# Hybrid decoder layer on one core: the order of small TensorE products between the wide weight products, and two moved steps around them

## The chip, the core and the metric

The kernel runs on one NeuronCore of a Trainium2 chip, in one launch. The metric is the device time of that core in microseconds (us), as the median of several runs.

## What is computed

One layer (DEPTH = 1) of a decoder, for 256 prompt tokens and 8 sample sequences of 4 tokens (32 sample tokens, so 288 token columns in all), with width 2048. Cut to what matters here:

```
proj = a @ w_in                                  # HGRN2 q,f,i,g | delta net q,k,v,z | gates
# HGRN2, 16 heads, chunks of 32 tokens, per chunk:
o = A @ i + (q*exp(G)) @ S ;  S = exp(G_last)*S + (k*exp(G_last-G))^T @ i
# gated delta net, 32 heads in 16 pairs, chunks of 64 tokens, per chunk:
X = solve(A + I, rhs)                            # triangular, unit diagonal
v_new = u - w @ S ;  o = (q*exp(gam)) @ S + attn @ v_new ;  S = exp(g_last)*S + k^T @ v_new
# then output projections, residuals, and a feed-forward part with w_up and w_down
```

The sample sequences start from given states (`state_hgrn`, `state_gdn`), so each head also has 8 products of one sample state with 4 tokens.

## The kernel before

All weights stream from HBM once. A weight piece of 128 x 512 is split by ScalarE into a rounded high part (`whi`, line 1036) and by VectorE into the rest (`wlo`, line 1530), and TensorE makes three products for each 128 x 128 tile of it: `whi` with the high part of the activations, `whi` with their low part, and `wlo` with the high part (lines 609, 610, 611), each 288 columns wide. These are called wide weight products here. SyncE issues the weight loads. A slab is 16 tiles of one block of 128 output rows, that is 48 wide weight products.

The small products of the two recurrences are put between them. `products` calls `between(s)` before every second tile, so a step s is followed by six wide weight products. One head of HGRN2 lasts four slabs (steps 0 to 31), one pair of delta-net heads six slabs (steps 0 to 47). While the projection of head i+1 is made, the steps of head i run (`hgrn_steps`, `delta_second`), together with those that prepare head i+1 (`delta_first`). ScalarE and VectorE have lists of steps by the same numbers (`delta_prev` and `delta_own` on each), with a split of a weight piece at every even step, in the order of the program. GpSimd (POOL) has its own order. So what an engine does is fixed by hand; semaphores say when.

All the small products have ordinary fp32 operands. Each shows in the trace as two MATMUL records and two LDWEIGHTS records; the two are called halves here. A transpose through TensorE shows one of each.

In the delta net the triangular inverse is built in levels. For level l = 1 to 5, TensorE makes PU (steps 4, 8, 11, 14, 17; line 799: the level's matrix with `g_Ui`), ScalarE copies it (line 1276), TensorE makes UT (steps 6, 10, 13, 16, 19; line 812: `g_PU` with `g_T`), VectorE subtracts it from `g_Ui` (line 1890) and transposes that to `g_T` (line 1893). PU of level l+1 waits for the subtraction of level l (`g_unew`). GpSimd makes the matrix of the level (`g_lev`, line 2338). At level 1 the samples have two 32 x 32 products more in PU (line 802) and in UT (line 815), subtracted in line 1889. Step 8 has four sample products of 32 columns (lines 823, 825), and steps 9 to 12 the sixteen of 8 columns with the sample states (line 833). When these are done (`g_sw`), GpSimd scales the states (line 2355, twice), after its level 5, which waits for PU of level 3. Step 16 starts with the sum of squares of the next head's keys or queries (line 742), which waits for ScalarE's square (line 1227) of what lines 1794 and 1795 on VectorE wrote; before these VectorE has line 1881, level 3 and the split of step 12.

In VectorE's step 5, `silu_z` (line 1872) multiplies two 128 x 288 arrays in SBUF for the output gate; in its own step 5 line 1774 copies the halo of the convolution (lines 1784 and 1787, step 10).

In HGRN2, step 0 transposes six blocks and makes the in-chunk products (lines 667, 668), step 10 the value products (683, 685), steps 11 to 14 the sixteen halves of 4 columns with the sample states (689), and steps 15 and 16 the chunk products (695).

## Time and profile before

| | |
|---|---|
| median of 3 runs | 3562.6 us (3562.56 to 3563.32) |
| the profiled execution's own time | 3563.5 us |
| its span from first to last instruction | 3562.0 us |
| mean granted TensorE clock | 0.994 |
| TensorE matmuls busy | 3481.4 us, 98% |
| TensorE weight loads busy | 3176.9 us, 89% |
| VectorE, ScalarE, GpSimd busy | 63%, 50%, 24% |
| HBM | 545.83 MB read, 40.99 MB written, 165 GB/s |

The profiled execution took 1.5 us more than its span, and stands 0.9 us above the median. The busy time of matmuls is modelled and overlaps from one to the next, so it doesn't say how much of it could go. The start times of the weight loads (engine PEld) do: in a stream of products there is one load for each product. HGRN2's heads run from about 187 to 745 us, the delta net's from about 998 to 1546 and from 1754 to 2350.

### The profile page before, as it was taken

Reading aid. Unit: us, or ns where it says so; the run is one execution under the profiler, and the core shown is the slowest. Engines: PE = TensorE matmul, PEld = TensorE weight load, DVE = VectorE, ACT = ScalarE, POOL = GpSimd, SP = SyncE. Lnnn points to the kernel's source line nnn. Section 1 sums busy time; section 2 is a strip of 40 time slices with the busy share of each in tenths; the row PEclk is TensorE's granted clock in tenths of the full one; section 3 lists DMA queues with packets and bytes.
Section 4 is the critical chain, followed back from the end, with each engine's and each line's share of the span. In section 5 each row is a group of like instructions: output and inputs, shape, how many; then the busy total and the mean of one; then the engine's idle time right before and its main releaser. Section 6 shows DMA issues by size and latency. Waiting matters only on the chain.

```text
span 3562.0 us, 76760 instructions
## 1 busy us (share of the span) xinstructions
PE 3481.4 (98%) x24605; PEld 3176.9 (89%) x24605; DVE 2252.7 (63%) x4307; ACT 1796.9 (50%) x3735; POOL 845.4 (24%) x995
## 2 busy tenths in 40 slices
PE   8999999999999999999999999999998999999998
PEld 2599999998889999998899999899878989999998
DVE  2476666746677777776677777646666665555555
ACT  1245454555545545556555555454665555444444
POOL 2122222201144554441244455412000000000000
PEclk9999999999999999999999999999999999999999
DMA  8655555568843433448744343468764785555554
GB/s 276 215 150 157 147 160 145 156 180 258 251 114 111 116 109 109 123 119 240 211 116 128 109 115 110 112 184 247 232 199 130 216 238 163 168 159 169 161 165 138
DMA packets 884546, 588.09 MB, mean 165 GB/s; under 512 B 23426, under 2 KB 816036, under 8 KB 884164
## 3 DMA queue, kind: packets, MB, share of 16 engines
q1 hardware_dynamic: 857828, 510.50, 50.0%
q0 software_dynamic: 26624, 76.41, 7.5%
q8 instruction: 50, 0.82, 0.1%
q14 instruction: 44, 0.36, 0.0%
HBM read 545.83 MB, written 40.99 MB: 165 GB/s over the span
## 4 chain that ended last, share of the span: by engine, by line
PE 93%; DVE 3%; issue 2%; DMA 1%; ACT 1%; DVEq 0%; POOL 0%; ACTq 0%; SPq 0%; POOLq 0%
PE acc L609 23%; PE acc L611 22%; PE acc L610 22%; PE acc L581 3%; PE bank L799 2%; PE bank L812 2%; PE bank L849 2%; PE bank L833 1%; PE bank L621 1%; PE bank L622 1%; DMA raw<-in_w_ada 1%; PE bank L870 1%; PE bank L674 1%; PE bank L676 1%; DVE wlo L1530 1%
## 5 line engine op out<-in xcount | busy, mean ns | idle before, releaser
L1530 DVE TENSOR_TENSOR wlo<-raw,whi 128x512 fp32r<-128x512 f32 x1799 | 1302.8, 742 | 828.9 <-ACT whi L1036 815.3
L1036 ACT ACTIVATE whi<-raw 128x512 fp32r<-128x512 f32 x1799 | 1094.8, 627 | 840.7 <-PE acc L611 799.5
L609 PE MATMUL acc<-ahi,whi 128*128 128x288 f32 x4112 | 1288.8, 313 | 14.5 <-DVE alo L2041 9.1
L610 PE MATMUL acc<-alo,whi 128*128 128x288 f32 x4112 | 1215.3, 296 | 0.0
L611 PE MATMUL acc<-ahi,wlo 128*128 128x288 f32 x4112 | 1211.4, 295 | 0.0
L609 PEld LDWEIGHTS acc<-ahi,whi 128*128 128x128 f32 x4112 | 775.5, 189 | 37.1 <-issue 26.2
L610 PEld LDWEIGHTS acc<-alo,whi 128*128 128x128 f32 x4112 | 776.6, 189 | 13.3 <-issue 11.5
L611 PEld LDWEIGHTS acc<-ahi,wlo 128*128 128x128 f32 x4112 | 775.9, 189 | 0.0
L609 PE MATMUL acc<-ohi,whi 128*128 128x288 f32 x1792 | 533.2, 298 | 3.9 <-ACT g_C L1045 3.3
L610 PE MATMUL acc<-olo,whi 128*128 128x288 f32 x1792 | 529.4, 295 | 0.0
L611 PE MATMUL acc<-ohi,wlo 128*128 128x288 f32 x1792 | 527.9, 295 | 0.0
L609 PEld LDWEIGHTS acc<-ohi,whi 128*128 128x128 f32 x1792 | 336.7, 188 | 22.6 <-DVE wlo L1530 10.0
L610 PEld LDWEIGHTS acc<-olo,whi 128*128 128x128 f32 x1792 | 337.0, 188 | 2.8
L611 PEld LDWEIGHTS acc<-ohi,wlo 128*128 128x128 f32 x1792 | 337.9, 189 | 0.0
L2338 POOL TENSOR_TENSOR g_lev<-g_A,levm 128x512 f32<-128x512 f32 x80 | 114.1, 1426 | 282.6 <-DVE g_C L1795 219.3
L1276 ACT ACTIVATE g_PU<-bank 128x512 f32<-128x512 f32 x80 | 47.8, 598 | 175.1 <-PE bank L799 164.4
L1787 DVE SCALAR_TENSOR_TENSOR g_ca<-g_U,g_cw,g_ca 128x312 f32<-128x312 f32 x192 | 131.8, 687 | 6.8
L581 PE MATMUL acc<-raw,cst 128*9 128x512 f32 x256 | 115.9, 608 | 7.0 <-DMA raw<-in_w_ada 4.4
L1890 DVE TENSOR_TENSOR g_Ui<-g_Ui,bank 128x512 f32<-128x512 f32 x80 | 54.7, 683 | 80.4 <-PE bank L812 80.4
L621 PE MATMUL bank<-whi,cs 128*18 128x512 f32 x256 | 101.3, 396 | 3.4 <-DVE wlo L1530 2.5
L799 PE MATMUL bank<-g_Ui,g_lev 128*128 128x128 f32 x640 | 87.9, 280 | 16.6 <-DVE g_Ui L1890 13.6
L581 PEld LDWEIGHTS acc<-raw,cst 128*9 128x9 f32 x256 | 22.4, 92 | 90.5 <-issue 70.7
(431 smaller groups left out, 4412.2 us busy)
## 6 DMA issues: line engine op xcount, KB each, us to landing
raw<-in_w_in SPq DMA_DIRECT2D x386, 512.0 KB, 4.1
raw<-in_w_ada SPq DMA_DIRECT2D x192, 512.0 KB, 4.6
raw<-in_w_up SPq DMA_DIRECT2D x128, 512.0 KB, 4.2
raw<-in_w_down SPq DMA_DIRECT2D x128, 512.0 KB, 4.0
raw<-in_w_out_gdn SPq DMA_DIRECT2D x64, 512.0 KB, 5.0
raw<-in_w_o SPq DMA_DIRECT2D x34, 512.0 KB, 4.7
raw<-in_w_out_hg SPq DMA_DIRECT2D x32, 512.0 KB, 5.5
g_S<-in_state_gdn POOLq DMA_DIRECT2D x32, 512.0 KB, 6.6
```

What stands on the lines that cost most here:

```text
L581: last = mm(acc[c % 2][0:NC, :], cst[:, 2 * l + a, :], raw[:, 2 * (l % 4) + a].rearrange("p k c -> p (k c)"), start=(l + a == 0), stop=(l ...
L609: mm(bank[:, 0:T], whi[:, s, r, :], hi[:, kt, :], start=(kt == 0), stop=False, skip_group_check=True)
L610: mm(bank[:, 0:T], whi[:, s, r, :], lo[:, kt, :], start=False, stop=False, skip_group_check=True)
L611: last = mm(bank[:, 0:T], wlo[:, s, r, :], hi[:, kt, :], start=False, stop=(kt == KT - 1), skip_group_check=True)
L621: mm(R[4][0:2 * NC, :], cs2[:, kt, :], whi[:, s].rearrange("p k c -> p (k c)"), start=(kt == 0), stop=False)
L799: last = mm(R[3][:, p * P:(p + 1) * P], glev[:, l % 2, p, :], gUi[:, p, :], start=True, stop=True)
L812: last = mm(R[2][:, p * P:(p + 1) * P], gT[:, p, :], gPU[:, p, :], start=True, stop=True)
L849: last = mm(R[4 + a][:, :], gkls[:, e, :], gvX[:, 4 * a:4 * a + 4, :].rearrange("p b v -> p (b v)"), start=True, stop=True)
L1036: f(whi[:, s], raw[:, r], ACT.Copy).then_inc(sg["hi_made"], 1)
L1530: tt_(wlo[:, s], raw[:, r], whi[:, s].bitcast(F32), SUB).then_inc(sg["lo_made"], 1)
L1787: stt(gca[:, 0:CW], gU[:, k, a:a + CW], gcw[:, k, a:a + 1], gca[:, 0:CW], MUL, ADD).then_inc(sg["g_part" if a < 3 else "g_tap"], 1)
L2338: last = pt(glev[:, l % 2], gA[:, :, :], levm[:, l, :].unsqueeze(1).to_broadcast([P, 4, P]), MUL)
```

## The change

It moves instructions; it adds and removes none but waits and signals. On TensorE:

- Level 1 of PU and of UT: the two 32 x 32 products, which were last, now stand after the first and after the second of the four large ones.
- The products of the decay matrices (step 31 of `delta_first`): the two products of 32 rows, which were last, now stand second.
- Step 0 of HGRN2: the 32 x 32 output block (line 668) and the two sample transposes now stand after the first transpose; the in-chunk products of the prompt end the step.
- The x transposes of the output stage: the one of 32 rows stands second of three.
- Step 8 of the delta net stands in front of PU of level 2 (it stood behind it).
- The sixteen products with sample states: ten halves at step 10 in front of UT of level 2, twenty-two at step 11 in front of PU of level 3 (before: 10, 6, 6, 10 halves at steps 9, 10, 11, 12, those of 10 and 11 behind the level product).
- HGRN2: all of step 10 to 14 in step 10, with a product of 128 columns last; steps 15 and 16 both in step 16.
- Step 37 of the delta net (output): one of the prompt's value products stands last, for each of the two heads.

On VectorE `silu_z` moves from step 5 to step 7. On GpSimd the first load of the sample states of the delta net (`load_delta(0)`) is issued after the last merged rows are stored, where it was before that loop.

```diff
 hgrn_steps, s == 0
                     for a in range(2):
                         turn(R[2][:, a * P:(a + 1) * P], hX[:, 3, a * P:(a + 1) * P], ident[:, :])
+                        if a == 0:
+                            mm(R[4][0:NS, TP:T], hX[:, 1, TP:T], hX[:, 0, TP:T], start=True, stop=True)
+                            turn(R[3][0:NS, 0:P], hX[:, 3, TP:T], ident[:, :])
+                            turn(R[3][0:NS, P:2 * P], hi_[:, TP:T], ident[:, :])
                         turn(R[2][:, (2 + a) * P:(3 + a) * P], hi_[:, a * P:(a + 1) * P], ident[:, :])
-                    turn(R[3][0:NS, 0:P], hX[:, 3, TP:T], ident[:, :])
-                    turn(R[3][0:NS, P:2 * P], hi_[:, TP:T], ident[:, :])
...
 hgrn_steps, s == 10
+                    pe.wait_ge(sg["h_s0"], 16 * (n + 1))
+                    mm(R[7][:, 0:P], htok[:, 2, :], hAT[:, 0:P], start=True, stop=False, skip_group_check=True)
                     mm(R[7][:, TP:T], htoks[:, 1, :], hAT[:, TP:T], start=False, stop=False, skip_group_check=True)
-                if s in (11, 12, 13, 14):
-                    pe.wait_ge(sg["h_s0"], 16 * (n + 1))
-                    for b in range(2 * s - 22, 2 * s - 20):
+                    for b in range(NB):
...
+                    mm(R[7][:, P:2 * P], htok[:, 3, :], hAT[:, P:2 * P], start=False, stop=False, skip_group_check=True)
-                if s in (15, 16):
-                    first, end = ((1, 5), (5, NHC))[s - 15]
-                    pe.wait_ge(sg["h_step"], 8 * n + end - 1)
+                if s == 16:
+                    pe.wait_ge(sg["h_step"], 8 * n + NHC - 1)
...
 delta_second: the step 8 block and the state products, now in front of PU and UT
+                if s in (10, 11):
+                    if s == 10:
+                        pe.wait_ge(sg["g_qw"], n + 1)
+                        pe.wait_ge(sg["g_s0"], 32 * (n + 1))
+                    for i in range(*((0, 5), (5, 2 * NB))[s - 10]):
...
                     for p in range(4):
                         last = mm(R[3][:, p * P:(p + 1) * P], glev[:, l % 2, p, :], gUi[:, p, :], start=True, stop=True)
-                    if l == 1:
-                        for e in range(2):
-                            last = mm(R[5][0:NS, e * NS:(e + 1) * NS], glevs[:, e, :], gUs[0:NS, e, :], start=True, stop=True)
+                        if l == 1 and p < 2:
+                            mm(R[5][0:NS, p * NS:(p + 1) * NS], glevs[:, p, :], gUs[0:NS, p, :], start=True, stop=True)
...
                     for p in range(4):
                         last = mm(R[2][:, p * P:(p + 1) * P], gT[:, p, :], gPU[:, p, :], start=True, stop=True)
-                    if l == 1:
-                        for e in range(2):
-                            last = mm(R[4][0:NS, e * NS:(e + 1) * NS], gTs[:, e, :], gPUs[:, e, :], start=True, stop=True)
+                        if l == 1 and p < 2:
+                            mm(R[4][0:NS, p * NS:(p + 1) * NS], gTs[:, p, :], gPUs[:, p, :], start=True, stop=True)
...
-                if s in (9, 10, 11, 12):
-                    if s == 9:
...
-                    for i in range(*((0, 5), (5, 8), (8, 11), (11, 2 * NB))[s - 9]):
...
 VectorE, delta_prev
-                if s == 5:
+                if s == 7:
                     silu_z(2 * n + 2, 1)
...
 GpSimd
-            load_delta(0)
             with pool.Fori(KT // 2 - 2, KT // 2) as n:
                 merged_out(n)
...
+            load_delta(0)
             pool.wait_ge(sg["g_halo_turned"], 1)
```

## Rows read from the trace of the kernel before

**Rows 1.** The page: busy us (share of the span) x instructions of TensorE.

```profile
PE 3481.4 (98%) x24605; PEld 3176.9 (89%) x24605; DVE 2252.7 (63%) x4307; ACT 1796.9 (50%) x3735; POOL 845.4 (24%) x995
```

**Rows 2.** Waits of TensorE: us in total, times, longest.

```profile
PE bank L799 <- DVE g_Ui L1890: 13.6, 15, 1.5
```

**Rows 3.** Timeline of the weight loads, step 12: start, us, instruction.

```profile
1331.68 1.21 PEld L833 LDWEIGHTS bank<-g_QW,g_S 128*128 128x128 f32 x10
1332.81 0.19 PEld L609 LDWEIGHTS acc<-ahi,whi 128*128 128x128 f32 x1
```

**Rows 4.** Timeline of the weight loads, step 6 (UT of level 1).

```profile
1318.39 0.99 PEld L812 LDWEIGHTS bank<-g_PU,g_T 128*128 128x128 f32 x8
1319.50 0.20 PEld L815 LDWEIGHTS bank<-g_PUs,g_Ts 32*32 32x32 f32 x4
1319.74 0.19 PEld L609 LDWEIGHTS acc<-ahi,whi 128*128 128x128 f32 x1
1319.84 0.19 PEld L610 LDWEIGHTS acc<-alo,whi 128*128 128x128 f32 x1
```

**Rows 5.** Timeline of the weight loads, HGRN2 step 0.

```profile
319.00 0.14 PEld L663 LDWEIGHTS bank<-ident,h_i 128*128 128x128 f32 x1
319.11 0.10 PEld L664 LDWEIGHTS bank<-ident,h_X 128*32 128x32 f32 x1
...
319.33 0.53 PEld L667 LDWEIGHTS bank<-h_X 128*128 128x128 f32 x4
319.98 0.14 PEld L668 LDWEIGHTS bank<-h_X 128*32 128x32 f32 x2
320.15 0.19 PEld L609 LDWEIGHTS acc<-ahi,whi 128*128 128x128 f32 x1
```

**Rows 6.** Timeline of VectorE, steps 4 to 6 of the same head as rows 4.

```profile
1318.26 1.78 DVE L1530 TENSOR_TENSOR wlo<-raw,whi 128x512 fp32r<-128x512 f32 x1 [2.06 <-ACT whi L1036]
1319.96 1.54 DVE L1872 TENSOR_TENSOR g_z<-g_ca,g_ce 128x288 f32<-128x288 f32 x1
...
1321.72 0.67 DVE L1890 TENSOR_TENSOR g_Ui<-g_Ui,bank 128x512 f32<-128x512 f32 x1
```

**Rows 7.** Timeline of the weight loads in front of step 8: same head, last head.

```profile
1321.18 0.19 PEld L611 LDWEIGHTS acc<-ahi,wlo 128*128 128x128 f32 x1
1322.50 0.30 PEld L799 LDWEIGHTS bank<-g_Ui,g_lev 128*128 128x128 f32 x2 [1.14 <-issue]
...
2280.02 0.19 PEld L611 LDWEIGHTS acc<-ahi,wlo 128*128 128x128 f32 x1
2281.90 0.30 PEld L799 LDWEIGHTS bank<-g_Ui,g_lev 128*128 128x128 f32 x2 [1.69 <-issue]
```

**Rows 8.** Timeline of GpSimd, levels 3, 4 and 5, then the state scaling.

```profile
1319.46 1.72 POOL L2338 TENSOR_TENSOR g_lev<-g_A,levm 128x512 f32<-128x512 f32 x1
...
1323.75 1.28 POOL L2338 TENSOR_TENSOR g_lev<-g_A,levm 128x512 f32<-128x512 f32 x1 [1.04 <-PE bank L799]
...
1330.60 1.58 POOL L2338 TENSOR_TENSOR g_lev<-g_A,levm 128x512 f32<-128x512 f32 x1 [1.80 <-PE bank L799]
1333.06 3.76 POOL L2355 TENSOR_TENSOR g_S<-g_S,g_sc 128x1024 f32<-128x1024 f32 x2 [0.88 <-PE bank L833]
```

**Rows 9.** Timeline of VectorE, steps 10 to 13.

```profile
1329.92 2.60 DVE L1787 SCALAR_TENSOR_TENSOR g_ca<-g_U,g_cw,g_ca 128x312 f32<-128x312 f32 x3
...
1334.80 0.69 DVE L1890 TENSOR_TENSOR g_Ui<-g_Ui,bank 128x512 f32<-128x512 f32 x1 [1.17 <-PE bank L812]
...
1336.16 1.21 DVE L1530 TENSOR_TENSOR wlo<-raw,whi 128x512 fp32r<-128x512 f32 x1
```

**Rows 10.** Timeline of the weight loads around step 16.

```profile
1338.15 0.19 PEld L611 LDWEIGHTS acc<-ahi,wlo 128*128 128x128 f32 x1
1338.57 0.30 PEld L742 LDWEIGHTS bank<-g_ns,ones 128*128 128x128 f32 x2 [0.23 <-issue]
```

**Rows 11.** VectorE in the last head's step 5, with no next head behind it.

```profile
2276.28 3.09 DVE L1872 TENSOR_TENSOR g_z<-g_ca,g_ce 128x288 f32<-128x288 f32 x1
```

More of the change, by code:

```diff
@@ L681, in hgrn_steps @@
                     pe.wait_ge(sg["h_t1"], n)
-                    for a in range(2):
-                        mm(R[7][:, a * P:(a + 1) * P], htok[:, 2 + a, :], hAT[:, a * P:(a + 1) * P], start=(a == 0), stop=False,
-                           skip_group_check=True)
+                    pe.wait_ge(sg["h_s0"], 16 * (n + 1))
+                    mm(R[7][:, 0:P], htok[:, 2, :], hAT[:, 0:P], start=True, stop=False, skip_group_check=True)
                     mm(R[7][:, TP:T], htoks[:, 1, :], hAT[:, TP:T], start=False, stop=False, skip_group_check=True)
-                if s in (11, 12, 13, 14):
-                    pe.wait_ge(sg["h_s0"], 16 * (n + 1))
-                    for b in range(2 * s - 22, 2 * s - 20):
+                    for b in range(NB):
                         mm(R[7][:, TP + b * TS:TP + (b + 1) * TS], hS0[:, b, :], hX[:, 2, TP + b * TS:TP + (b + 1) * TS],
                            start=False, stop=False, skip_group_check=True)
-                if s in (15, 16):
-                    first, end = ((1, 5), (5, NHC))[s - 15]
-                    pe.wait_ge(sg["h_step"], 8 * n + end - 1)
-                    for c in range(first, end):
+                    mm(R[7][:, P:2 * P], htok[:, 3, :], hAT[:, P:2 * P], start=False, stop=False, skip_group_check=True)
+                if s == 16:
+                    pe.wait_ge(sg["h_step"], 8 * n + NHC - 1)
+                    for c in range(1, NHC):
                         last = mm(R[7][:, c * HC:(c + 1) * HC], hS[:, c - 1, :], hX[:, 2, c * HC:(c + 1) * HC], start=False,
                                   stop=(c == NHC - 1), skip_group_check=True)
-                    if s == 16:
-                        last.then_inc(sg["h_o"], 1)
+                    last.then_inc(sg["h_o"], 1)
                 if s == 19:
@@ L788, in delta_second @@
                     last.then_inc(sg["g_qk_turned"], 1)
+                if s == 8:
+                    pe.wait_ge(sg["g_unew"], 5 * n + 1)
+                    pe.wait_ge(sg["g_tokd"], EARLIER + n + 1)
+                    pe.wait_ge(sg["g_halo"], halos)
+                    for e in range(2):
+                        mm(R[7][:, e * NS:(e + 1) * NS], gbek[:, 2, e, :], gUs[:, e, :], start=True, stop=True)
+                    for e in range(2):
+                        last = mm(R[7][:, 64 + e * NS:64 + (e + 1) * NS], gbv[:, 2, e, :], gUs[:, e, :], start=True, stop=True)
+                    last.then_inc(sg["g_uts"], 1)
+                if s in (10, 11):
[3 more added lines that the diff above has]
+                    for i in range(*((0, 5), (5, 2 * NB))[s - 10]):
+                        e, b = i // NB, i % NB
+                        last = mm(R[4][:, 64 * e + 8 * b:64 * e + 8 * b + 8], gS0[:, e, b, :],
+                                  gQW[:, e, b].rearrange("p k t -> p (k t)"), start=True, stop=True)
+                    if s == 11:
+                        last.then_inc(sg["g_sw"], 1)
                 if s in PU:
@@ L890, in delta_second @@
                         bank = (R[7], R[4])[e]
-                        for a in range(2):
-                            mm(bank[:, a * P:(a + 1) * P], gvn[:, a, e, :], gat[:, a, e, :], start=(a == 0), stop=False, skip_group_check=True)
+                        mm(bank[:, 0:P], gvn[:, 0, e, :], gat[:, 0, e, :], start=True, stop=False, skip_group_check=True)
                         mm(bank[:, TP:T], gvns[:, e, :], gats[:, e, :], start=False, stop=False, skip_group_check=True)
                         for c in range(1, NGC):
-                            last = mm(bank[:, c * GC:(c + 1) * GC], gS[:, c - 1, e, :], gqpT[:, e, c * GC:(c + 1) * GC],
-                                      start=False, stop=(c == NGC - 1), skip_group_check=True)
+                            mm(bank[:, c * GC:(c + 1) * GC], gS[:, c - 1, e, :], gqpT[:, e, c * GC:(c + 1) * GC],
+                               start=False, stop=False, skip_group_check=True)
+                        last = mm(bank[:, P:2 * P], gvn[:, 1, e, :], gat[:, 1, e, :], start=False, stop=True, skip_group_check=True)
                     last.then_inc(sg["g_o"], 1)
@@ L938, in x_turn @@
                         for a in range(2):
-                            turn(R[5 + k % 2][:, a * P:(a + 1) * P], xin[:, a, c], ident[:, :])
-                        turn(R[5 + k % 2][:, TP:T], xin[0:NS, 2, c], ident[0:NS, 0:NS]).then_inc(sg["w_xturned"], 1)
+                            last = turn(R[5 + k % 2][:, a * P:(a + 1) * P], xin[:, a, c], ident[:, :])
+                            if a == 0:
+                                turn(R[5 + k % 2][:, TP:T], xin[0:NS, 2, c], ident[0:NS, 0:NS])
+                        last.then_inc(sg["w_xturned"], 1)
                 for k in range(MIXED_SLABS):
```

29 lines of the change are left out of this document (7 added, 22 removed).

## The prediction

> **What bounds the kernel now.** I read the page first, then TensorE's waits, then, where the change is, the timelines of the weight loads, VectorE and GpSimd. On the page TensorE's matmuls are busy 98% of the span and VectorE 63% [rows 1]. So each slot on TensorE counts, and work elsewhere counts only where TensorE waits for it. The list of waits has one line that bears on the change: 13.6 us in 15 waits of L799 for L1890 [rows 2]. Busy time can't tell what an order of products costs, since matmul records overlap; the starts of the weight loads can, as each product has one. I take them as the clock of TensorE.
>
> **Narrow products, and bursts of them.** Ten loads of L833, each for a product of only 8 columns, take 1.13 us up to the next load [rows 3]: 0.113 us each. The eight of L812, 128 columns wide, go at the same pace: the eighth starts some 0.78 us after the first [rows 4]. So a narrow product costs one load, 0.11 us, whatever is in front of or behind it. A burst that ends with 8 columns leaves the next wide weight product's load visible; one that ends with 128 columns has the load under the product, but takes 0.11 us for it as well. In rows 3 the wide product's load follows the last narrow one like any other. I cost at nothing: HGRN2's steps 10 to 16, the sixteen state products put in two bursts, the wide product last in step 37, and the order in step 31 and of the x transposes, which have one change of shape before and one after. If a boundary of a burst has a cost that I miss, say 0.01 us, it is 16 x 7 boundaries, 1 us, of either sign. The wide product that now signals step 37's end is 64 columns longer than L895's, half of a 0.11 us slot, 0.05 us; step 40 waits for what follows from it, so 16 x 0.05 = +0.8 us.
>
> **The 32-row products.** In UT of level 1 the eighth L812 load would start at 1318.39 + 0.13 + 6 x 0.112 = 1319.19 and the next at 1319.30, but L815's starts at 1319.50: 0.20 us late. Its four halves follow each other 0.03 us apart, and L609's load comes 0.24 us after the first. L610's follows 0.10 us later, a load that nothing covers [rows 4]. Without L815, L609 would start at 1319.30 and not at 1319.74: the four halves cost 0.43 to 0.44 us. The same shape of cost stands in HGRN2, for two halves: the last of four L667 loads starts at about 319.66, L668's should follow at 319.77, and L609's comes at 320.15 [rows 5], so 0.38 us for two. So most of the cost is the change of shape, once in and once out, and not the product: two halves more add 0.06 us. The change puts the pair of the first head behind the first large product and that of the second behind the second, with a large one between: two changes in and two out. Two pairs apart cost 2 x (0.435 - 0.06) = 0.75 us, against 0.435: +0.315 us. With PU and UT of level 1 in 16 head pairs, 32 x 0.315 = **+10.1 us**. Bounds: nothing, if the change of shape is free inside a burst; 2 x 0.38 - 0.435 = 0.33 us by HGRN2's row, +10.6 us. I take the first, as it has the same shape. Nothing hides it: UT's end sets level 1's subtraction, and TensorE has work up to it.
>
> The Trainium skill (TensorE: Matmul & The Clock Gate, Step-by-step: what each phase is for) says that a weight load is pulled ahead of matmuls in flight if the row groups don't conflict or the load goes to the background buffer. By that the 32-row load would go under the large product, and this term would be 0. The late L815 load [rows 4] speaks against it here.
>
> In HGRN2's step 0 the number of changes stays one, but behind L668 comes L664, with 32 columns to load in place of 128. L664 follows L663 with no gap, 0.11 us [rows 5]. The exposed load behind L668 should shrink from 0.10 to about 0.03 us, the pace of the 32-column loads of L815: 15 x -0.07 = -1.1 us, between that and 0.
>
> **Step 8 and silu_z.** In front of step 8's L799, the last wide load is at 1321.18; L799's is due at 1321.31 and comes at 1322.50: a gap of 1.19 us [rows 7]. It waits for L1890, 1321.72 to 1322.39, which stood behind L1872, in VectorE's queue: 1319.96 to 1321.50 [rows 6]. L1872 reads two arrays in SBUF and took 1.54 us, as POOL's L2338 ran to 1321.18 [rows 8]. With L1872 in step 7, VectorE has only the halo copy between the split that ends at 1320.04 and UT's end. UT ends about 0.63 us later by the term above (0.315 twice), at about 1320.4. From L1872's end to L1890's, halo copy included, are 0.89 us (1321.50 to 1322.39), so L1890 ends by 1321.3, and L799 is due at 1321.31 + 0.63 = 1321.94. The gap goes, with 0.6 us to spare. The load starts show such a gap in 13 heads, 0.87 to 1.22 us, 14.8 us in all, and in two heads none; the list's 13.6 us [rows 2] counts idle time from modelled ends, some 0.25 us short for each. In the last head the gap is 1.75 us [rows 7]: there L1872 took 3.09 us [rows 11] and the split of step 6 stands behind it; some 1.5 of it should go. Sum **-16.3 us**. Bounds: 0 if L1890 is held by something else, -17.5 by the list with 0.26 added to each wait. The step 8 products now stand in front of L799 and wait for the same signal, so this order alone would gain nothing. L1872 is next used at step 42; in its new place it is behind the split of step 6, and the pieces are three ahead.
>
> **Level 3 and step 16.** What is late next is GpSimd. Now L2338 of level 5 starts at 1330.60 when PU of level 3 is done, and the scaling L2355 waits for the last state product, 1333.06 to 1336.82 [rows 8]. VectorE's split of step 12 reads two SBUF arrays; it starts at 1336.16 and ends at 1337.37, 0.55 us after L2355 ends, and took 1.21 in place of 0.69 [rows 9]. L1794, L1795 and L1227 follow, and L742 of step 16, due at 1338.28, comes at 1338.57 [rows 10]. So TensorE already waits 0.29 us there, and a later end of L2355 is paid in full. After the change PU of level 3 stands behind 22 halves and not 6: relative to UT of level 2, 16 x 0.112 = 1.79 us later. L2338 starts at 1332.39. VectorE's three L1787 (2.60 us, the last held by L2338 [rows 9]) are then done, so it takes 1.28 us as in level 4 [rows 8], to 1333.67. The signal for L2355 is there already; two of 1.90 us (3.76 overlapped) end at 1337.43: 0.6 us later than 1336.82, while UT of level 3, which VectorE's split follows, stays where it is. L742 has a next head in 15 heads: 15 x 0.58 = **+8.7 us**. Bounds: 0 if the split gets in between the two L2355, and 15 x 1.0 if L2338 takes 1.72. I take the middle, since the split is asked for in the middle of the second L2355, before as after.
>
> The Trainium skill (SBUF — State Buffer, Who interferes with whom) says that a VectorE instruction with two SBUF inputs and a GpSimd one that reads SBUF hold each other off for a whole instruction. With that rule the wait lasts to the end of the second L2355, as in my sum; if they only shared bandwidth, the term would be nearer to 2 us.
>
> The other levels keep their waits: between UT and the next PU of levels 3 and 4 there is one step before as after. UT of level 3 now has only 12 wide products between it and PU, for ScalarE's copy, as UT of level 1 has before too, and that one comes without a gap [rows 2, 4]. HGRN2's step 16 waits for VectorE's last state step, which the list of waits doesn't show now, and it is put no earlier. load_delta(0) is issued later, but its states are first used in step 10 of the second stretch of six slabs, 6 x 48 x 0.13 = 37 us after the first: 0.
>
> **Sum.** +0.8 + 10.1 - 1.1 - 16.3 + 8.7 = +2.2 us, with some 0.5 for boundaries +2.7. Against the profiled execution's 3563.5 us (span 3562.0 and 1.5 around it) that is 3566.2; the median before is 0.9 lower, so **3565.3 us**.
>
> **Rivals.** (a) The second change of shape is free: without the 10.1, 3555.2. For it: no row shows a 32-row product in front of a large fp32 one. Against: L609's load behind L815 waits for the same thing. (b) No later L742: without the 8.7, 3556.6. For it: it rests on when two queues meet. (a) and (b) together: 3546.5. (c) Slower: L2338 of level 5 starts at 1332.39, and VectorE's split of step 10 at about 1331.7 (0.9 earlier than L1787's end now, without the hold), done at 1332.4. If it starts later than L2338, they meet, L2338 takes 1.58 to 1.72 us as in rows 8, and L742 comes 0.3 to 0.44 us later still: +4.5 to +6.6 us, 3569.8 to 3571.9. It decides from 0.3 us on. (d) The gap at step 8 stays because L1890 is held by L2338 itself and not through L1872: 3565.3 + 16.3 = 3581.6. Against: L1890 took 0.69 us at 1334.80 while L2355 ran [rows 8, 9]. (e) The change does nothing that can be seen since its parts cancel: that is nearly my forecast.
>
> **Chances.** 0.2% is 7.1 us, about what a measurement of this kernel can tell from no change. My forecast 0.42, (a) 0.14, (b) 0.15, (a) with (b) 0.06, (c) 0.16, (d) 0.03, others 0.04. Faster by over 0.2% (below 3555.5): (a), both, some of the forecast's and (b)'s lower side, 0.27. Slower (above 3569.7): (c), (d) and a part of the forecast's upper side, 0.22. The same: 0.51. The range leaves out (a) with (b), and (d): 3551 to 3573; my forecast's own is 3560 to 3570.
>
> **What the profile after would show.** L799's wait for L1890 near nothing, and L1872 at 0.45 us. L802 and L815 in groups of two, each behind a gap of 0.2 us, and 0.37 us for each. L2355 ending 0.6 us later against UT of level 3, and L742's gap at 0.87 us in place of 0.29. If L742 comes no later or a group of two costs under 0.1 us, I am too high; if L799 still waits at step 8, too low.

## The result, and the profile after

The changed kernel takes 3574.5 us (median of 7 runs, 3570.9 to 3576.1) where the kernel before takes 3562.6 (7 runs, 3558.7 to 3566.6). The ratio is 1.0032, with an interval of 1.0020 to 1.0043: 11 to 12 us slower, where I had forecast 3565.3, no measurable change, and a range of 3551 to 3573. The profiled execution took 3570.9 us with a span of 3569.4, so it is the fastest of the seven, 7.4 us above the one before. Of the executions of all the kernels below, one stood apart (h0_back, 3641.8 us at a mean granted clock of 0.916), and its ratio leaves it out.

The page's busy row, to set beside [rows 1]:

```profile
PE 3491.1 (98%) x24605; PEld 3181.5 (89%) x24605; DVE 2213.3 (62%) x4307; ACT 1793.7 (50%) x3735; POOL 848.2 (24%) x995
```

Instruction counts are the same; VectorE is busy 40 us less: 17 of it are L1872, which no longer meets L2338, 15 the convolution (L1787) and 12 the splits, which meet GpSimd less often too, and other lines have a little more. TensorE's waits, as in [rows 2] (line numbers are those of the changed kernel: L818 is PU, old L799; L740 is old L742; L676 is old L674; L899 is old L901):

```profile
PE bank L740 <- ACT g_ns L1227: 6.4, 11, 0.6
...
PE bank L676 <- POOL h_iXs L2201: 3.8, 13, 0.3
PE bank L899 <- DVE wlo L1530: 3.5, 14, 0.3
...
PE bank L818 <- DVE g_Ui L1890: 2.0, 2, 1.4
```

Of the 15 waits of [rows 2] those at step 8 are gone. Of the two left for L1890, both in the last head, one of 0.7 us was there before, and one of 1.4 us is new (see below). L740's wait is the one I had forecast. The waits of L676 and L899 I had not.

**Level 1.** The weight loads of step 6, the same head as [rows 4]:

```profile
1324.46 0.32 PEld L830 LDWEIGHTS bank<-g_PU,g_T 128*128 128x128 f32 x2
1324.90 0.13 PEld L832 LDWEIGHTS bank<-g_PUs,g_Ts 32*32 32x32 f32 x2
1325.08 0.30 PEld L830 LDWEIGHTS bank<-g_PU,g_T 128*128 128x128 f32 x2
1325.49 0.13 PEld L832 LDWEIGHTS bank<-g_PUs,g_Ts 32*32 32x32 f32 x2
1325.67 0.52 PEld L830 LDWEIGHTS bank<-g_PU,g_T 128*128 128x128 f32 x4
1326.11 0.19 PEld L609 LDWEIGHTS acc<-ahi,whi 128*128 128x128 f32 x1
```

From the first load to the last group of four are 1.21 us, of which the four large loads in between are 0.45: 0.76 for two pairs apart, where four halves together cost 0.435 [rows 4]. L832 comes some 0.2 us late both times, behind large products of its own burst.

**Step 8.** VectorE has only the split and the halo copy in front of UT's end; its timeline:

```profile
1326.71 0.67 DVE L1890 TENSOR_TENSOR g_Ui<-g_Ui,bank 128x512 f32<-128x512 f32 x1
1327.41 0.71 DVE L1893 STREAM_TRANSPOSE g_T<-g_Ui 128x512 f32<-128x512 f32 x1
1328.05 0.65 DVE L1530 TENSOR_TENSOR wlo<-raw,whi 128x512 fp32r<-128x512 f32 x1
1328.62 0.45 DVE L1872 TENSOR_TENSOR g_z<-g_ca,g_ce 128x288 f32<-128x288 f32 x1
```

L1890 is done at 1327.38, before the first product of step 8 is due at 1327.67, and that comes on time. L1872 takes 0.45 us and not 1.54 [rows 6].

**Step 16.** GpSimd's levels 4 and 5 and its scaling, as in [rows 8]:

```profile
1329.83 1.29 POOL L2338 TENSOR_TENSOR g_lev<-g_A,levm 128x512 f32<-128x512 f32 x1 [1.33 <-PE bank L818]
...
1337.58 1.28 POOL L2338 TENSOR_TENSOR g_lev<-g_A,levm 128x512 f32<-128x512 f32 x1 [2.69 <-PE bank L818]
1338.83 3.74 POOL L2355 TENSOR_TENSOR g_S<-g_S,g_sc 128x1024 f32<-128x1024 f32 x2
```

and the loads around L740, as in [rows 10]:

```profile
1343.36 0.19 PEld L611 LDWEIGHTS acc<-ahi,wlo 128*128 128x128 f32 x1
1344.33 0.30 PEld L740 LDWEIGHTS bank<-g_ns,ones 128*128 128x128 f32 x2 [0.78 <-issue]
```

L740 is due at 1343.49 and comes at 1344.33: a gap of 0.84 us, 0.29 before. Level 5's L2338 takes 1.27 to 1.29 us in all 16 heads, where it took 1.58 to 1.61 in 15 of them before: the meeting of rival (c) doesn't come.

**Step 14 of the last head** takes 1.3 us longer (3.52 and not 2.22), which I had not forecast. Behind the moved state products GpSimd's scaling now starts 0.22 us ahead of VectorE's split of step 12, where before it started 0.34 us behind it:

```profile
2301.82 4.20 POOL L2355 TENSOR_TENSOR g_S<-g_S,g_sc 128x1024 f32<-128x1024 f32 x2
```

```profile
2302.04 2.22 DVE L1530 TENSOR_TENSOR wlo<-raw,whi 128x512 fp32r<-128x512 f32 x1 [4.23 <-ACT whi L1036]
```

```profile
2305.11 0.97 PEld L818 LDWEIGHTS bank<-g_Ui,g_lev 128*128 128x128 f32 x8 [1.59 <-DVE wlo L1530]
```

The split takes 2.22 us and not 0.69, the subtraction of level 3 (L1890) stands behind it, and PU of level 4 (L818) waits for that. states_only below has the same 1.3 us.

**HGRN2, the first surprise.** Per head, step 8 of HGRN2 takes 4.36 us in 13 of 16 heads, the third to the fifteenth (from the first product of one step's weight stream to that of the next), and 3.83 in all but the first before. Here are GpSimd and then VectorE in such a head (the fifth) of the kernel before:

```profile
321.92 2.49 POOL L2199 TENSOR_TENSOR h_iX<-h_tok,cm 128x512 f32<-128x512 f32 x2 [5.73 <-ACT h_toks L1135]
324.37 1.89 POOL L2201 TENSOR_TENSOR h_iXs<-h_toks,cm 32x1024 f32<-32x1024 f32 x1
```

```profile
322.81 0.70 DVE L1530 TENSOR_TENSOR wlo<-raw,whi 128x512 fp32r<-128x512 f32 x1 [0.47 <-ACT whi L1036]
324.42 3.80 DVE L1530 TENSOR_TENSOR wlo<-raw,whi 128x512 fp32r<-128x512 f32 x3 [0.90 <-ACT whi L1036]
```

and in the changed kernel:

```profile
322.20 2.49 POOL L2199 TENSOR_TENSOR h_iX<-h_tok,cm 128x512 f32<-128x512 f32 x2 [5.74 <-ACT h_toks L1135]
324.65 2.39 POOL L2201 TENSOR_TENSOR h_iXs<-h_toks,cm 32x1024 f32<-32x1024 f32 x1
```

```profile
322.99 0.79 DVE L1530 TENSOR_TENSOR wlo<-raw,whi 128x512 fp32r<-128x512 f32 x1 [0.38 <-ACT whi L1036]
324.59 0.69 DVE L1530 TENSOR_TENSOR wlo<-raw,whi 128x512 fp32r<-128x512 f32 x1 [0.80 <-ACT whi L1036]
```

Before, L2201 starts 0.05 us ahead of the split of step 4 and the split is held. After, the split starts 0.06 us ahead of L2201, and L2201 is the one that is held: 2.39 us and not 1.89. The product of step 8 (L676), which waits for it, is 0.5 us late. Step 0 became 0.09 us shorter, as forecast (-0.07); the split follows the products of the first slab and so comes that much earlier, while L2201 hangs on ScalarE's copies and doesn't. Counted from the last wide load ahead of step 0, the split starts after 5.80 us and not 5.89, and L2201 after 5.85 us in both kernels. In the second head of the same execution the order is still the old one (L2201 starts 0.04 us ahead, takes 1.89), and its step 8 takes 3.83.

**The clock, the second surprise.** Windows of the changed kernel: stretch, us, busy time of TensorE, weight loads, VectorE, ScalarE, GpSimd (instructions), granted clock, DMA share, GB/s. The first two are of the third delta net head, the other two of the fifth:

```profile
1182.40:1185.90 3.50, 3.50 (x33) 3.50 (x33) 3.36 (x7) 0.00 (x0) 1.02 (x2) 1.00 0.60 181
1185.90:1189.30 3.40, 3.40 (x16) 3.40 (x16) 0.27 (x2) 2.66 (x6) 3.19 (x3) 0.50 0.00 0
1333.90:1337.40 3.50, 3.50 (x33) 3.50 (x33) 3.36 (x7) 0.00 (x0) 0.99 (x2) 1.00 0.59 178
1337.40:1340.80 3.40, 3.36 (x27) 3.12 (x26) 1.00 (x4) 2.66 (x6) 3.22 (x3) 1.00 0.00 0
```

Both heads run the eleven state products of step 11 (22 halves of 8 columns) and PU of level 3 in the first stretch, at a granted clock of 1.00, 2.4 GHz, with TensorE busy throughout. In the third head the next 3.4 us are granted 0.50, 1.2 GHz, and hold 16 products, in the fifth 27. This happens in three heads here (3, 4 and 7) and in none of the kernel before at that place. Heads with a fall take 11.8 us for steps 9 to 13 and those without 10.2: +1.56 us. Step 16 gives 0.82 of it back, since GpSimd doesn't slow down and L740 then waits for nothing (2.08 and not 2.90 us), so a fall costs 0.74 us net.

**Step 40** takes 0.20 us longer in each head: L899's waits in the list above.

### The profile page after: what moved, and what is told of

Its sections match the earlier page's. It is cut to its first block, busy times and chain, and to the rows that moved or that the text cites. A ratio compares the mean times of both kernels' runs of the same rounds, so it can differ in the third digit from the quotient of the medians.

```text
span 3569.4 us, 76730 instructions
## 1 busy us (share of the span) xinstructions
PE 3491.1 (98%) x24605; PEld 3181.5 (89%) x24605; DVE 2213.3 (62%) x4307; ACT 1793.7 (50%) x3735; POOL 848.2 (24%) x995
## 4 chain that ended last, share of the span: by engine, by line
PE 63%; DVE 5%; issue 2%; ACT 1%; DVEq 0%; ACTq 0%
PE acc L609 16%; PE acc L611 15%; PE acc L610 15%; PE bank L830 2%; PE bank L818 2%; DVE wlo L1530 2%; PE bank L847 2%; PE bank L804 2%; PE bank L621 1%; PE bank L622 1%; DVE g_ca L1787 1%; PE bank L770 1%; ACT whi L1036 1%; PE bank L740 0%; PE bank L879 0%
## 5 line engine op out<-in xcount | busy, mean ns | idle before, releaser
L2338 POOL TENSOR_TENSOR g_lev<-g_A,levm 128x512 f32<-128x512 f32 x80 | 109.7, 1371 | 305.4 <-DVE g_C L1795 223.4
L1787 DVE SCALAR_TENSOR_TENSOR g_ca<-g_U,g_cw,g_ca 128x312 f32<-128x312 f32 x192 | 116.6, 607 | 6.8
L818 PE MATMUL bank<-g_Ui,g_lev 128*128 128x128 f32 x640 | 99.3, 291 | 4.5 <-DVE g_Ui L1890 2.0
L1890 DVE TENSOR_TENSOR g_Ui<-g_Ui,bank 128x512 f32<-128x512 f32 x80 | 54.6, 683 | 79.1 <-PE bank L830 79.1
L622 PE MATMUL bank<-wlo,cs 128*18 128x512 f32 x256 | 101.4, 396 | 0.0
```

The lines of the kernel that those rows point to most:

```text
L622: mm(R[4][0:2 * NC, :], cs2[:, kt, :], wlo[:, s].rearrange("p k c -> p (k c)"), start=False, stop=(kt == KT - 1)).then_inc(sg["piece_used" ...
L818: last = mm(R[3][:, p * P:(p + 1) * P], glev[:, l % 2, p, :], gUi[:, p, :], start=True, stop=True)
L1787: stt(gca[:, 0:CW], gU[:, k, a:a + CW], gcw[:, k, a:a + 1], gca[:, 0:CW], MUL, ADD).then_inc(sg["g_part" if a < 3 else "g_tap"], 1)
L2338: last = pt(glev[:, l % 2], gA[:, :, :], levm[:, l, :].unsqueeze(1).to_broadcast([P, 4, P]), MUL)
```

## The experiments

All ratios are to the kernel before on the same chip. "Falls" are the delta net heads whose step 11 is followed by a stretch at half clock in the profiled execution.

| kernel | median us | ratio (interval) | falls |
|---|---|---|---|
| changed kernel | 3574.5 | 1.0032 (1.0020 to 1.0043) | 3 |
| h0_only | 3566.9 | 1.0015 (1.0005 to 1.0024) | 0 |
| h0_wide_behind | 3568.4 | 1.0016 (1.0007 to 1.0026) | 0 |
| h0_back | 3564.1 | 1.0006 (0.9996 to 1.0016) | 2 |
| silu_only | 3543.9 | 0.9949 (0.9932 to 0.9966) | 0 |
| level1_back | 3567.1 | 1.0012 (1.0002 to 1.0022) | 12 |
| out37_back | 3572.4 | 1.0028 (1.0018 to 1.0038) | 4 |
| states_back | 3561.6 | 1.0000 (0.9990 to 1.0009) | 0 |
| states_only | 3573.8 | 1.0034 (1.0022 to 1.0047) | 2 |
| d31_back | 3568.6 | 1.0018 (1.0009 to 1.0027) | 10 |
| h0_late_split | 3565.5 | 1.0005 (0.9996 to 1.0015) | 4 |
| states_between | 3575.8 | 1.0034 (1.0022 to 1.0046) | 4 |
| silu_states3 | 3543.6 | 0.9941 (0.9927 to 0.9954) | 0 |

### HGRN2's step 0: four kernels

**h0_only**: the kernel before with the new order of step 0 alone.

```diff
+                        if a == 0:
+                            mm(R[4][0:NS, TP:T], hX[:, 1, TP:T], hX[:, 0, TP:T], start=True, stop=True)
+                            turn(R[3][0:NS, 0:P], hX[:, 3, TP:T], ident[:, :])
+                            turn(R[3][0:NS, P:2 * P], hi_[:, TP:T], ident[:, :])
```

(and the same three lines taken out behind the loops; the last of the prompt's in-chunk products now gives the signal `h_turned`, which L668's gave.)

> The kernel before with only the new order of HGRN2's step 0. The trace of the changed kernel shows a new wait of 0.55 us at step 8 (L676 for POOL's L2201) in 13 heads, in a part that was costed at -1.1 us. Theory A: the step is 0.08 us shorter (a load of 32 columns and not of 128 is exposed behind the 32-column product), so the weight pieces and VectorE's split come 0.08 us earlier against POOL's chain, which hangs on the start of the step; the split now starts 0.05 us before POOL's L2201 and not 0.05 us after it, and POOL is held by it. Expects all of the HGRN2 stretch's +6.6 us here, about +6.5 us in total. Theory B: the wait comes from the merged steps 10 to 16, through the state of the next head. Expects about -1 us here.

Measured: step 8 of HGRN2 0.53 us longer in 13 heads, HGRN2's heads 2 to 16 together +5.7 us, the rest of the kernel as before; 1.0015. The new order of step 0 brings the wait by itself.

**h0_wide_behind**: as h0_only, but only the sample product goes in front; the two 32-column transposes stay last.

> The kernel before with L668's product second in HGRN2's step 0 as in the change, but with a transpose of 128 columns behind it, the two sample transposes later. Theory A (0.08 us shorter step turns the order of the split and L2201 round): the exposed load is of 128 columns again, the step as long as before, so the wait at step 8 goes: 0 against before. Theory C: the signal h_turned comes later against the wide products, as the last product of the step is a large one: the wait at step 8 stays, +6.5 us.

Measured: the wait stays (step 8 +0.53 us in the same way, the heads +6.2 us). The price of an exposed load is not what counts. The first wide load comes 1.58 us after the last one ahead of step 0, against 1.63 before and 1.54 in the changed kernel: 0.05 us earlier is enough for the split to start first (5.83 us behind that last load). The later signal that the expectation weighs has no part in it: L2201 starts 5.85 us behind that load here as in the kernel before.

**h0_back**: the changed kernel with step 0 as before.

> The changed kernel with HGRN2's step 0 in the old order. Theory A: no wait at step 8, the HGRN2 stretch as long as before the change (within 0.5 us), so 6.5 us less than the changed kernel, about +4 us against before. Theory B (merged steps 10 to 16): the wait stays, about +11 us against before.

Measured: the wait is gone and step 8 takes 3.83 us. The heads are +0.95 us against before, 0.06 each, which is what is left of the change in HGRN2: its steps 10 to 16, whose products are in fewer bursts.

**h0_late_split** asks the port alone. All orders on TensorE are those of the changed kernel, and VectorE gets an instruction more:

```diff
+                    if s == 4 and n is not None:
+                        k = s // 2 + AHEAD
+                        dve.wait_ge(sg["hi_made"], at.pieces_before(k) + 1)
+                        dve.wait_ge(sg["piece_used"], atleast0(at.pieces_before(k) - SPLIT + 1))
+                        nc.vector.memset(hpad[:, :], 0.0)
```

> The changed kernel with one more instruction and nothing else: in HGRN2, VectorE fills a small unused tile (128 x 64) right in front of the split of step 4, after the split's own waits, so that the split starts some 0.1 us later. In the changed kernel this split starts 0.06 us before GpSimd's L2201 in heads 3 to 15, L2201 takes 2.39 us and L676 of step 8 waits; where it starts 0.04 us after L2201, as in head 2 and in the kernel before, L2201 takes 1.89 us and nothing waits. Theory, the order at the shared port is the whole cause: the split falls behind L2201 again, step 8 goes back from 4.36 to 3.83 us in 13 heads, -6.5 us against the changed kernel, about 3568, with an instruction more. Rival, the wait comes from the order on TensorE itself (a later product or signal): step 8 stays at 4.36 us and the time at 3574.5.

Measured: GpSimd and VectorE in the same head as above:

```profile
323.34 2.49 POOL L2205 TENSOR_TENSOR h_iX<-h_tok,cm 128x512 f32<-128x512 f32 x2 [5.73 <-ACT h_toks L1136]
325.80 1.89 POOL L2207 TENSOR_TENSOR h_iXs<-h_toks,cm 32x1024 f32<-32x1024 f32 x1
```

```profile
325.79 0.11 DVE L1716 MEMSET h_pad<- 128x64 f32 x1 [0.86 <-ACT whi L1037]
325.85 2.39 DVE L1531 TENSOR_TENSOR wlo<-raw,whi 128x512 fp32r<-128x512 f32 x1
```

The split (L1531 here) now starts 0.05 us behind L2207 (old L2201), which takes 1.89 us. The thirteen heads are 0.50 us shorter each, -6.55 us together, as expected, and the ratio falls from 1.0032 to 1.0005. (That is 9.6 us, more than the heads show; the intervals, 0.001 to either side, allow for both.) A useless instruction of 0.11 us takes 6.5 us off HGRN2's heads: which of the two starts first is nearly the whole of this cost, 0.50 of 0.53 us a head. The Trainium skill (SBUF — State Buffer, Who interferes with whom) says that the ports which VectorE and GpSimd share are locked and not divided. These rows agree: whoever starts first takes its usual time (0.69 or 1.89 us), and the other's is longer by about what is left of it.

### silu_z alone

**silu_only**: the kernel before with `if s == 5:` of silu_z as `if s == 7:`.

> The kernel before with only L1872 moved from VectorE's step 5 to step 7. By the prediction's step the gap of 1.2 us in front of step 8 goes in 13 heads, and most of 1.75 us in the last: -16 us against before. The rival (L1890 is held by POOL's L2338 itself) expects 0 to -5 us. That the gap only moves to a later wait of the same head would show as a total near 0 with L799's wait gone.

Measured: 0.9949, -18 us. TensorE's waits for L1890 at step 8, 13.6 us in 15 waits [rows 2], are down to

```profile
PE bank L799 <- DVE g_Ui L1890: 0.7, 1, 0.7
```

By the starts of the products, the gap is worth 14.5 us in the first fifteen heads and 1.46 in the last, 16.0 in all, where I had 16.3. This one line is all that helps in the change. The profiled span is shorter by another 3.1 us in the last head, where the profiled execution of before had 6.8 us at a low clock behind the gap; h0_only keeps the gap and has no such stretch, so it doesn't belong to the gap alone.

### The parts of the delta net

**level1_back**: the changed kernel with the 32x32 products of level 1 last again.

```diff
-                        if l == 1 and p < 2:
-                            mm(R[5][0:NS, p * NS:(p + 1) * NS], glevs[:, p, :], gUs[0:NS, p, :], start=True, stop=True)
+                    if l == 1:
+                        for e in range(2):
+                            last = mm(R[5][0:NS, e * NS:(e + 1) * NS], glevs[:, e, :], gUs[0:NS, e, :], start=True, stop=True)
```

(the same in UT.)

> The changed kernel with the four 32x32 products of level 1 last in their step again, in PU and UT, all else as changed. My sum: each of the 32 steps is 0.315 us shorter (one change of shape in place of two), -10.1 us against the changed kernel, so about 3564.4 by the medians; steps 4 and 6 by 0.3 us each per head in the load starts, and the gap in front of step 8 stays under 0.3 us. Rival, the second change of shape is not what costs 0.33 us a step in the changed kernel: steps 4 and 6 stay as long as they are and the time stays at 3574.

Measured: steps 4 and 6 are 0.33 us shorter each in every head, less 0.03 that steps 5 and 7 take back: the term stands. But the clock falls in 12 heads and not in 3, which at 0.74 us net takes some 6.7 us back in the profiled execution, whose span is 4.5 us shorter than the changed kernel's. The ratio is 1.0012 against 1.0032, -7 us. Why the clock falls so much more often in this kernel isn't shown.

**states_only** and **states_back**: the kernel before with only the sixteen state products moved (five in front of UT of level 2 in step 10, eleven in front of PU of level 3 in step 11), and the changed kernel with them as before. The move, as the first makes it:

```diff
+                if s in (10, 11):
...
+                    for i in range(*((0, 5), (5, 2 * NB))[s - 10]):
...
-                if s in (9, 10, 11, 12):
...
-                    for i in range(*((0, 5), (5, 8), (8, 11), (11, 2 * NB))[s - 9]):
```

> The kernel before with only the sixteen state products moved: five in front of PU of level 3 (step 10), eleven in front of UT of level 3 (step 11). By my sum +8.7 us (GpSimd's scaling ends 0.6 us later and step 16 waits for it in 15 heads). Theory with the clock: windows of half clock at step 11 in some heads add 1 to 1.3 us each, +9 to +13 in all. Rival, the move is free without the rest of the change (the gap in front of step 8 shifts nothing here, so GpSimd would have to be ahead of it): 0 to +2.

> The changed kernel with the sixteen state products behind the level's products in steps 9 to 12, as before. Theory, the burst has two costs: the scaling on GpSimd ends later, so that the product of step 16 waits 0.55 us more a head in 15 heads (-8.3 us if undone, and the wait for the copy back to about 0.3 us or to nothing), and the 22 narrow halves in a row let the granted clock fall to half in some heads at step 11 (three windows in the profile, 3 to 4 us if undone, and no window there). Together -8 to -12 us: 3562 to 3566. Rival, the clock windows have nothing to do with the burst: they stay at some heads, and the gain is -8 us at most.

Measured for states_only: 1.0034. Step 16 takes 2.90 us where it took 2.35, +0.55 in the heads without a fall (8.3 us if it were all 15), step 14 of the last head takes 1.3 us longer, and the clock falls in two heads. The move alone costs as much as the whole change. (The expectation has the places wrong: five products stand in front of UT of level 2 and eleven in front of PU of level 3.)

Measured for states_back: 1.0000, so 11 us of the change's cost go with the move undone. Step 16 is back at 2.35 us in every head, and the clock falls in none. It could have gained more: its step 9 is 0.35 us longer in each head. There the copy of g_QW stands behind the copy of PU in ScalarE's queue, whose product step 8 now signals last, and the state products of step 9 wait for it. In the changed kernel these stand in step 10, and this wait doesn't show.

**states_between**: the eleven products of step 11 three by three between the large ones of PU.

```diff
                     for p in range(4):
+                        if s == 11:
+                            last = states(5 + 3 * p, min(8 + 3 * p, 2 * NB))
```

> The changed kernel with the eleven state products of step 11 between the four products of PU of level 3 (3, 3, 3 and 2 of them in front of each 128-column one) in place of all in front of it: the same work, the same end of the level product, no more than six narrow halves in a row. A fall of the granted clock at step 11 costs 1.56 us there and gives 0.82 us back at step 16, where TensorE then doesn't wait: 0.74 us net. Theory, a long row of narrow halves is what lets the clock fall: no half-clock stretch in the delta net, steps 9 to 13 at 10.2 us in all heads, and about 4 us less than the changed kernel by the medians, 3570 to 3572. Rival, it is the amount of narrow work near step 11, however it is cut: stretches of half clock stay in 3 to 12 heads.

Measured: the clock falls in four heads (1, 8, 10 and 11). My theory fell: that the narrow halves stand in one row is not what lets it fall. What the eight kernels with a fall share is eleven state products in step 11; the five others and the kernel before, with at most six in one step, show none. The kernel is also 0.32 us a head slower, since the state products now stand behind PU's wait for the level's subtraction, which they covered (only the profiled executions show this; the ratio, 1.0034, hardly differs from the changed kernel's 1.0032):

```profile
1185.22 0.74 PEld L801 LDWEIGHTS bank<-g_QW,g_S 128*128 128x128 f32 x6 [0.29 <-issue]
1185.89 0.30 PEld L822 LDWEIGHTS bank<-g_Ui,g_lev 128*128 128x128 f32 x2
1186.11 0.75 PEld L801 LDWEIGHTS bank<-g_QW,g_S 128*128 128x128 f32 x6
```

**out37_back** and **d31_back**: the changed kernel with step 37, or step 31, as before.

```diff
-                        if a == 0:
-                            mm(R[4][0:NS, 384:448], smask[:, :], gGRs[:, 0].rearrange("p e s -> p (e s)"), start=True, stop=True)
-                            mm(R[4][0:NS, 448:512], m_str_s[:, :], gGRs[:, 1].rearrange("p e s -> p (e s)"), start=True, stop=True)
...
+                    mm(R[4][0:NS, 384:448], smask[:, :], gGRs[:, 0].rearrange("p e s -> p (e s)"), start=True, stop=True)
+                    mm(R[4][0:NS, 448:512], m_str_s[:, :], gGRs[:, 1].rearrange("p e s -> p (e s)"), start=True,
+                       stop=True).then_inc(sg["g_d"], 1)
```

> The changed kernel with step 37 as before (both wide products in front, the narrow state products last). In the profile of the changed kernel the stretch of step 40 is 0.21 us a head longer than before, where I had summed 0.05 for the longer last product. If that order is the whole cause, -3.4 us against the changed kernel (16 x 0.21); if only the length of the last product counts, -0.8 us and 0.16 us a head stay, from ScalarE's split standing in front of its copy; if the order has no part in it, 0.

> The changed kernel with step 31 as before (the two 64-column products of the samples last, and they signal). The kernels with step 37 or the state products as before keep step 40 0.20 us a head longer, so the cause should be the signal of step 31, which now hangs on a 256-column product: ScalarE's copies of the decays (L1205) start 0.28 us later after it, and its queue carries that to the copy of step 40. If so, step 40 is 0.20 us a head shorter in 16 heads, -3.2 us against the changed kernel, about 3571. Rival: the order of step 31 has no part in it, step 40 stays as it is, and the time stays at 3574.5.

Measured: out37_back leaves step 40 as long as in the changed kernel, so step 37 has no part in it. With d31_back step 40 is 0.20 us shorter in every head: the cause is the signal of step 31. ScalarE in the changed kernel, behind the last load of step 31, at 1370.91:

```profile
1371.54 1.08 ACT L1205 ACTIVATE g_GR<-bank 128x512 f32<-128x512 f32 x2 [2.34 <-PE bank L757]
```

and in d31_back, where the last loads are those of the 32-row products:

```profile
1368.66 1.09 ACT L1204 ACTIVATE g_GR<-bank 128x512 f32<-128x512 f32 x2 [2.15 <-PE bank L756]
```

The first weight load of the stream behind the step is at 1371.13 in the changed kernel and at 1368.55 in d31_back, so the copy starts 0.41 us behind it in the one and 0.11 in the other. Of these 0.30 us 0.10 are the stream's own load, which comes earlier; counted from the stream ahead of the step, the copy starts 0.20 us later (3.36 and not 3.16). The step is as long, but what signals it is a product of 256 columns and not one of 64. The 0.20 us are carried to step 40 by VectorE's queue and not by ScalarE's, whose second split behind the copy is on time again. In this head VectorE's split behind the copy is 0.19 us later, and so are all its instructions up to L1787, which ScalarE waits for. The copy L1304, which step 40's chain hangs on, is then 0.20 us later. The ratio is 1.0018, some 5 us less than the changed kernel, though the clock falls in ten heads of its profiled execution.

### A version that beats both

**silu_states3**: silu_only with the state products behind the level products of three steps, not four.

```diff
-                if s in (9, 10, 11, 12):
+                if s in (9, 10, 11):
...
-                    for i in range(*((0, 5), (5, 8), (8, 11), (11, 2 * NB))[s - 9]):
+                    for i in range(*((0, 5), (5, 10), (10, 2 * NB))[s - 9]):
```

> The kernel before with silu_z in step 7 and the sixteen state products behind the level products of three steps (5, 5 and 6 in steps 9, 10 and 11) in place of four: GpSimd's scaling may start about 0.7 us earlier, when L2338 is done. Theory: the wait for the copy of step 16 (2.35 us where 2.08 is without a wait) goes, -0.27 us in 15 heads, -4 us against silu_z in step 7 alone, which gave 0.9949 of before: about 0.9938, 3540. Rivals: another wait holds step 16, no gain (0.9949); or 12 narrow halves in a row already let the clock fall in some heads, +1.5 us each.

Measured: 3543.6 us, 0.9941 (0.9927 to 0.9954), 18 us below the kernel before on that chip. Step 16 is 0.27 us shorter in 15 heads, as expected: the scaling on GpSimd is early enough. But 0.18 comes back in step 14, whose PU now waits for VectorE's subtraction:

```profile
PE bank L799 <- DVE g_Ui L1890: 4.6, 16, 0.7
```

That leaves 0.07 us a head, 1 us, less than these runs can tell from silu_only. The clock falls in no head, with six state products in step 11.

## Why the prediction was wrong

The terms, with what the profiled executions show (starts of products, step by step):

| term | predicted us | measured us |
|---|---|---|
| level 1, the pairs apart | +10.1 | +9.4 (16 x (0.66 - 0.07)) |
| HGRN2 step 0 itself | -1.1 | -1.4 (15 x 0.09) |
| HGRN2 step 8, L676's wait | 0 | +6.9 (13 x 0.53) |
| HGRN2 steps 10 to 16 | 0 | +0.9 (15 x 0.06) |
| step 8's gap | -16.3 | -16.0 |
| step 16, L742 later | +8.7 | +8.3 (15 x 0.55) |
| step 40 | +0.8 (step 37) | +3.2 (16 x 0.20, from step 31) |
| step 14 of the last head | 0 | +1.3 |
| half clock behind step 11 | 0 | +2.2 (3 x 0.74), more in other runs |

Their measured sum is +14.8. The span grew by 7.4 only. The profiled execution of before had 3.1 us of its own at half clock in its last head, the stages that the change doesn't touch came out 2.9 us shorter in sum (the start, the first HGRN2 head and the stretch behind HGRN2; they differ by as much among kernels that are equal there), and two waits of single heads, at steps 2 and 30, are 1.7 us shorter.

**The step that failed** is the one on HGRN2's step 0: "The exposed load behind L668 should shrink from 0.10 to about 0.03 us [...] 15 x -0.07 = -1.1 us, between that and 0." The load did shrink so. But I asked what a shorter step saves and not what an earlier VectorE meets. L2201 and the split of step 4 stood 0.05 us apart in the trace of before, and the gain moved the split past it: +6.9 us, outside the bounds that I gave. With this step put back, or the split held 0.1 us, the kernel takes 1.0006 and 1.0005 of before (h0_back, h0_late_split), some 2 us more where I had forecast 2.7. That these come so near is in part luck, as both still have the terms below that I had at nothing or too low. In the delta net I had weighed the same kind of meeting, as rival (c), where L2338 took 1.28 us as forecast, since the split of step 10 ended 0.16 us ahead of it (so (c) failed too, though its 3569.8 to 3571.9 us lie nearest to what was measured); in HGRN2 I read no row of VectorE or GpSimd, because the change touched no instruction of theirs.

**Right, with its size**: level 1 (0.59 us a head against 0.63), the gap of step 8, and the gap in front of L740 (0.84 against 0.87 forecast), each shown by a kernel that undoes or does it alone. Rivals (a), (b) and (d) are refuted by level1_back, states_only and silu_only. The Trainium skill's rule on loads pulled ahead (TensorE: Matmul & The Clock Gate, Step-by-step: what each phase is for), by which level 1 would have cost nothing, is not borne out by these rows: L832 comes 0.2 us late behind a large product of its own burst.

**Wrong in cause**: step 40. I looked at the length of the last product of step 37, which has slack, and passed over step 31, with "one change of shape before and one after". What counted there was which product signals: the copy on ScalarE starts 0.20 us later, and VectorE's queue carries that to step 40.

**Missing**: the last head's step 14 and the clock. I had weighed the meeting of the split of step 12 and L2355 for the heads in which L2355 starts first before as after [rows 8, 9]; in the last head their order turned round, as in HGRN2.

On the clock: "I cost at nothing" fits the burst's own length, which is as forecast: 22 loads from 1333.84 to 1336.32, 0.113 us each. That the burst brings falls of the clock is shown by states_only (2) and states_back (0), with everything else the same. How many falls an execution has is not settled: 2 to 12 in the eight kernels profiled. The other six runs of the changed kernel have a mean granted clock of 0.991 to 0.992 where the profiled one has 0.993 and is 0.5 to 5 us faster, which would fit some more of them; they have no trace, so that is an estimate.

**Open**: what makes the clock fall in one head and not in the next, though both ran the same products in front of it; and whether ten state products in a step would bring it, as only 3 to 6 and 11 were tried. A version with level 1 and step 31 as before and the state products put apart was not run; by the terms above, it would be silu_only.

## What to carry to other kernels

A step that gets shorter moves the engine behind it, and if two engines meet at a shared port within 0.1 us, the order can flip and cost many times what the step saved. So list the near meetings of VectorE and GpSimd in each stage that a change touches, also where it touches only TensorE. A reordered burst has three prices besides its length: the changes of array shape (0.38 us for two 32-row halves, way in and way back), which product signals, and what waits for that signal on slower engines.

## What the runs showed of the hardware

- 0.11 us of VectorE work without use, put in front of a split, took 6.5 us off thirteen heads, as GpSimd's instruction then starts first: a shift of 0.05 us decides whether GpSimd's takes 1.89 or 2.39 us.
- The granted clock fell to half for 3.4 us behind a stretch in which TensorE had been busy all the time (3.50 of 3.50 us) and had run 22 halves of 8 columns and eight of 128. It came in 2 to 12 of 16 heads in eight kernels, also with the narrow halves cut into rows of six, and in none of the kernels with at most twelve such halves in the step.
- A fall costs less than it seems: of 1.56 us, 0.82 came back at the next wait for GpSimd, whose pace doesn't change.
- A pair of 32-row halves costs 0.38 us between 128-row products of a burst (0.76 for two pairs) as well as at its end (HGRN2's step 0, [rows 5]).
